# A Strassen-form decoder block in split float32: V and first group in turns, Silu on ScalarE, residuals added by DMAs

## The reference

```python
hn = rmsnorm(x, norm_g)
u_a, v_a, z_a, h_b, gb, gc, z_b = split(hn @ w_in)          # 1024 x 3584
out_a = u_a * (w_s_masked @ layernorm(v_a) + b_s) * silu(z_a)   # per chunk of 128, 4 heads
out_b = gb * causal_conv3(gc * h_b) * silu(z_b)
x = x + concat(out_a, out_b) @ w_out                         # 1024 x 1024
gate = sigmoid(rmsnorm(x, ple_norm_g) @ w_ple_gate)          # 1024 x 1024
x = x + gate * (p @ w_ple_proj)                              # 256 x 1024
out = rmsnorm(x, final_g)
```

## Time and profile before

| | |
|---|---|
| median of 3 runs | 1079.71 us (1077.2 to 1080.1) |
| the profiled execution: its time, its span | 1078.01 us, 1076.3 us |
| granted TensorE clock, mean | 0.966 of full speed |
| TensorE busy | 967.0 us (90%), 4646 matmuls |
| VectorE busy | 818.5 us (76%), 1227 instructions |
| ScalarE busy | 463.6 us (43%), 705 |
| GpSimd busy | 1.6 us, 10 |
| DMA | 94.15 MB, 87 GB/s over the span |

### The profile page before, as it was taken

The page is one execution under the profiler, slowest core; times in us unless marked ns, Lnnn a source line. Parts: engine busy times, 40 slices in busy tenths (PEclk is TensorE's granted clock), DMA queues, the critical chain, the costliest instruction groups (busy, mean ns, idle before and its releaser), DMA issues. The chain is left out here.

```text
span 1076.3 us, 12830 instructions
## 1 busy us (share of the span) xinstructions
PE 967.0 (90%) x4646; PEld 807.5 (75%) x4646; DVE 818.5 (76%) x1227; ACT 463.6 (43%) x705; POOL 1.6 (0%) x10
## 2 busy tenths in 40 slices
PE   2689999999998899889949999999999889989992
PEld 2589788888887678678749978888888767877871
DVE  3587987776779965787699898876767997578568
ACT  5454433333333414866745443333333342476351
POOL 0000000000000000000000000000000000000000
PEclk9689999999999999999979999999999999998997
DMA  9100111321213146303731122113121214510325
GB/s 304 48 1 28 52 40 40 82 75 41 78 40 118 40 156 234 145 13 117 218 134 40 43 61 55 40 53 104 40 79 40 98 59 157 194 40 1 118 79 195
DMA packets 76958, 94.15 MB, mean 87 GB/s; under 512 B 5985, under 2 KB 57697, under 8 KB 76897
## 3 DMA queue, kind: packets, MB, share of 16 engines
q1 hardware_dynamic: 76896, 93.35, 26.6%
HBM read 76.56 MB, written 16.78 MB: 87 GB/s over the span
## 5 line engine op out<-in xcount | busy, mean ns | idle before, releaser
L407 PE MATMUL banks<-ring_hi,slot 128*128 128x512 f32 (+1 forms) x672 | 248.5, 370 | 51.6 <-DVE ring_lo L1048 32.5
L1048 DVE TENSOR_TENSOR ring_lo<-work,ring_hi 128x512 fp32r<-128x512 f32 (+1 forms) x204 | 172.3, 846 | 143.8 <-ACT ring_hi L707 142.9
L407 PE MATMUL banks<-slot,ring_hi 128*128 128x512 f32 x672 | 264.3, 393 | 7.2 <-DVE work L1201 7.2
L408 PE MATMUL banks<-slot,ring_hi 128*128 128x512 f32 x672 | 261.7, 389 | 0.0
L409 PE MATMUL banks<-slot,ring_lo 128*128 128x512 f32 x672 | 261.7, 389 | 0.0
L707 ACT ACTIVATE ring_hi<-work 128x512 fp32r<-128x512 f32 (+1 forms) x204 | 153.5, 754 | 241.7 <-PE banks L409 221.8
L408 PE MATMUL banks<-ring_lo,slot 128*128 128x512 f32 (+1 forms) x672 | 244.5, 364 | 0.0
L409 PE MATMUL banks<-ring_hi,slot 128*128 128x512 f32 (+1 forms) x672 | 244.4, 364 | 0.0
L407 PEld LDWEIGHTS banks<-ring_hi,slot 128*128 128x128 f32 x672 | 132.9, 198 | 77.0 <-DVE ring_lo L1048 38.4
L407 PEld LDWEIGHTS banks<-slot,ring_hi 128*128 128x128 f32 x672 | 126.1, 188 | 39.7 <-DVE work L1201 13.9
L409 PEld LDWEIGHTS banks<-ring_hi,slot 128*128 128x128 f32 x672 | 132.5, 197 | 18.7
(11 more groups left out here) (101 smaller groups left out, 894.0 us busy)
## 6 DMA issues: line engine op xcount, KB each, us to landing
work<-in_w_in_dram SPq DMA_DIRECT2D x48, 512.0 KB, 5.1
slot_raw<-in_x_dram SPq DMA_DIRECT2D x16, 512.0 KB, 5.7
side<-in_x_dram SPq DMA_DIRECT2D x8, 1024.0 KB, 5.0
work<-in_w_out_dram SPq DMA_DIRECT2D x8, 1024.0 KB, 5.1
work<-in_w_ple_gate_dram SPq DMA_DIRECT2D x8, 1024.0 KB, 6.7
x_dram<-keep SPq DMA_DIRECT2D x16, 512.0 KB, 6.5
side<-x_dram SPq DMA_DIRECT2D x16, 512.0 KB, 3.9
out_dram<-keep SPq DMA_DIRECT2D x16, 512.0 KB, 3.0
```

The lines of the kernel that those rows point to most:

```text
L407: pe.matmul(ps, left_hi, right_hi, start=OPENS[q] and c == 0, stop=False, skip_group_check=on)
L408: pe.matmul(ps, left_hi, right_lo, start=False, stop=False, skip_group_check=on)
L1048: dve.tensor_tensor(ring_view(ring_lo, stage, place), ring_raw(stage, at, q), ring_view(ring_hi, stage, place).bitcast(F32), ALU.subtract) ...
```

## The change

- The Strassen products are signed anew: the operand's forms S1 to S4 have the same number of sums, but they are made in the order S3, S2, S4, S1, from other quarters at first (S3 = A11 - A21, S2 = A22 - S3, S4 = A12 - S2, S1 = A21 + A22), and `low_op` waits for other sums. Raw quarters lie in other slots.
- V and the first group run in turns: T(0,0), T(0,1), V0, V1, T(0,2..6), V2..6, then groups 1 to 11. The ring's places come from a table over this order (SEQ). The spatial weights move behind T(0,2) and T(0,5). The four mixing heads move to later pieces.
- V's products lie two tiles to a bank; copies and additions take 128x512 at a time, half as many.
- ScalarE computes Silu instead of Sigmoid in T (`gate_t`), VectorE drops the multiplication by z. G keeps Sigmoid.
- In O, ScalarE copies the products 0, 2, 3 (`copy_o`) and GpSimd adds x by accumulating DMAs; product 6 is still added by VectorE, to a quarter of x that SP has loaded in place. In P, x1 is added by accumulating DMAs in all 8 tiles of block 0 and in 4 of block 1; the other four are reloaded into slots.
- The weights of P have buffers of their own, outside the ring, and land in two halves. Block 1's weights and x are loaded at other points; block 0's outputs are stored by SP at the head of block 1's list.
- The last scalings (`y_tile`) are deferred: block 0's into block 1's T(0,2..5) and V2..5, block 1's to tiles 6 and 7. The two root chains of x1 become one.

The core of the diff:

```diff
-RAW_SLOT = {"A11": S2, "A12": S4, "A21": S3, "A22": A22}
+RAW_SLOT = {"A11": S3, "A12": S4, "A21": S1, "A22": A22}
-MIX_AFTER = {(2, 2): 0, (2, 6): 1, (3, 3): 2, (4, 2): 3}
+MIX_AFTER = {(2, 6): 0, (3, 2): 1, (3, 6): 2, (4, 3): 3}
+SEQ = [("T", 0, 0), ("T", 0, 1), ("V", 0), ("V", 1)] + [("T", 0, q) for q in range(2, 7)] + [("V", q) for q in range(2, 7)]
+SEQ += [("T", g, q) for g in range(1, NG) for q in range(PRODUCTS)]
+SEQ += [(stage, q, kk) for stage in "OG" for q in range(PRODUCTS) for kk in range(2)]
...
+        ADDED_BY_DMA = (8, 4)
...
             for b in range(BLOCKS):
+                if b:
+                    for i in range(TILES):
+                        sp.wait_ge(x2_step, X2("y", b - 1, i))
+                        sp.dma_start(out_tiles[b - 1, i], nat(i)).then_inc(out_stored[i], 16)
+                sp.wait_ge(w_lo_ready, W_LO("V", b, 4))
+                group_w(b, 1)
...
+                sp.wait_ge(op_lo_ready, OP_LO("mix", b, A11, 1))
+                sp.wait_ge(op_sum_ready, OP_SUM("mix", b, S3, 1))
+                sp.dma_start(nat_quarter(1, 0), x_half[b, 1][:, :, 0:HALF]).then_inc(x_quarter_landed, 16)
...
+            def add_x(b, q):                      # GpSimd's list
+                n, (t, h) = {0: (0, (0, 0)), 2: (1, (0, 1)), 3: (2, (1, 1))}[q]
+                pool.wait_ge(bank_copied, COPIED("O", b, q, 3))
+                for js in (slice(0, 2), slice(2, 4)):
+                    pool.dma_start(nat_quarter(t, h)[:, js, :], x_half[b, t][:, js, h * HALF:(h + 1) * HALF],
+                                   accum_op=ALU.add).then_inc(x_added[n], 16)
+            def add_x1(b, i):
+                pool.wait_ge(x1_stored[i], (b + 1) * 16)
+                pool.wait_ge(x2_step, X2("pp", b, i, 1))
+                pool.dma_start(nat(i), x1_tiles[b, i], accum_op=ALU.add).then_inc(x1_added[i], 16)
...
-                act.activation(sig_of(t), source, ACT.Sigmoid).then_inc(sigmoid_ready, SIGMOID.up(kind, b, i, t))
+                act.activation(gate_of(t), source, ACT.Silu).then_inc(gate_ready, GATE.up(kind, b, i, t))
...
+            def copy_o(b, q):
+                t, h = {0: (0, 0), 2: (0, 1), 3: (1, 1)}[q]
+                for s in {0: (S4,), 2: (S1, S2), 3: (S1, S3)}[q]:
+                    act.wait_ge(op_sum_ready, OP_SUM("mix", b, s, 1))
+                if q < 3:
+                    act.wait_ge(op_lo_ready, OP_LO("mix", b, A22 if q == 2 else A12, 1))
+                for j in range(4):
+                    act.wait_ge(product_done, PRODUCT("O", b, q, j))
+                    act.activation(nat(4 * t + j, h), banks[:, 4 + j if q == 3 else j, :], ACT.Copy)
...
+                gate_g(b, 1, 0)                   # ScalarE, seam
+                if b < last:
+                    for i in range(4, TILES):
+                        squares_x(b + 1, i)
+                    raw_x(b + 1, "A11")
+                    split_w(b + 1, ("T", 0, 0))
+                    raw_x(b + 1, "A12")
...
+                        if n == 5:                # VectorE, O and G
+                            add_natural(b, stage, 1)
+                        if n == 10:
+                            add_natural(b, stage, 4)
+                        if n == 12:
+                            add_natural(b, stage, 5)
...
+                        if g == 0 and q in (2, 3, 4, 5):     # VectorE, T
+                            for kk in range(2):
+                                low_op("hn", b, {2: S1, 3: S3, 4: S4, 5: A22}[q], kk)
+                        if b and g == 0 and q in (2, 4):
+                            rstd_of_squares(C_X2 + 2 * q - 4, C_X2 + 2 * q, "x2", b - 1, 2 * q - 1, q // 2 - 1)
+                        if b and g == 0 and q in (2, 3, 4, 5):
+                            y_tile(b - 1, q - 2, 0)
...
+                if i >= ADDED_BY_DMA[b]:          # x2_tile
+                    dve.wait_ge(x1_again_landed[i], 16)
+                    dve.wait_ge(x2_step, X2("pp", b, i, 1))
+                    dve.tensor_tensor(nat(i), nat(i), slot_tile(i), ALU.add).then_inc(x2_step, X2.up("sum", b, i))
```

More of the change, by code:

```diff
@@ L380, in loads @@
+            for i in range(TILES):
+                sp.wait_ge(x2_step, X2("y", last, i))
+                sp.dma_start(out_tiles[last, i], nat(i)).then_inc(out_stored[i], 16)
             for i in range(TILES):
@@ L630, in products @@
-                if b < last:
-                    x_fills(b + 1, "A11")
+                    elif stage == "O":
+                        _, q, kk = piece
+                        natural(b, "O", q, (2 * kk, 2 * kk + 1), "mix")
+                        if (q, kk) == (6, 0):
+                            x1_fills(b, "A11")
+                        if (q, kk) == (6, 1):
+                            x1_fills(b, "A12")
+                    else:
+                        _, q, kk = piece
+                        natural(b, "G", q, (2 * kk,), "x1")
+                        if (q, kk) == (0, 0):
+                            x1_fills(b, "A22")
+                        natural(b, "G", q, (2 * kk + 1,), "x1")
+                        if (q, kk) == (0, 0):
+                            x1_fills(b, "A21")
+                        if (q, kk) == (6, 0):
+                            p_fills(b)
@@ new lines, in raw_x1 @@
+            def raw_x1(b, name):
+                if b == 0 and name == "A11":
+                    act.wait_ge(const_landed, 16 * 6)
+                act.wait_ge(product_done, PRODUCT("O", b, RAW_SLOT[name], 3))
+                for c in range(4):
+                    act.wait_ge(x1t_done, X1T(b, name, c))
+                    k = 4 * QUARTERS[name][1] + c
+                    act.activation(op_raw(RAW_SLOT[name])[:, c, :], banks[:, 4 + c, :], ACT.Copy,
+                                   scale=ple_c[:, k:k + 1]).then_inc(raw_t_ready, RAW_T.up("x1", b, name, c))
@@ L860, in scalar_program @@
             act.wait_ge(pool_set, 1)
-            act.activation(warm[:, 1:2], warm[:, 0:1], ACT.Sigmoid)
+            act.activation(warm[:, 1:2], warm[:, 0:1], ACT.Silu)
             for i in range(4):
                 squares_x(0, i)
-            split_w(0, "V", 0)
-            for c in range(4):
-                raw_x(0, "A11", c)
+            split_w(0, ("T", 0, 0))
+            split_w(0, ("T", 0, 1))
+            for i in range(4, 6):
+                squares_x(0, i)
+            raw_x(0, "A11")
```

1606 lines of the change are left out of this document (765 added, 841 removed).

## The result

The changed kernel takes **1062.6 us** (median of four runs, 1060.2 to 1065.9) against 1079.9 for the kernel before on the same chip: a ratio of 0.985, 95% interval 0.982 to 0.988. It is faster, by 17 us, half of the 36 that 1044 meant. The profiled execution spans 1064.2 us, 12.1 less than the 1076.3 before.

What follows compares the result with a forecast made beforehand. TensorE's own work sets the floor; only its lost time, mostly waits for VectorE, can be won. Start -10, T -2, O -14, G -8, seam -4, end -1, table loads and hand-offs +5: -34, so 1044 us (1030 to 1056, chance 0.56).

Steps and rivals of the forecast that it cites:

- T: T stretch of each block: nearly full already, lighter gates take the waits at groups 1 and 11; -1 us per block.
- G: G stretch: 12.3 and 10.2 us lost before, waits of 1.4 and 4.5 us left; -4 us per block, near 88 each.
- O: O stretch: 10 us lost per block before, 3 left; -7 us per block, near 83 each.
- Start and end: Start: V and group 0 end about 102 us, -10. End: 22 us behind TensorE's last work, last P and end -1.
- Seam: From G's end in block 0 to V6's end in block 1: near 105 us from 108.6, -4, the least certain term.
- POOL: GpSimd's queue of added accumulating DMAs: landings of 5 to 8.6 us, priced 0; bounds 0 and 35 us.
- rival B: Accumulating DMAs come late, so the addition at half piece 10 delays TensorE; 1097 us at 35 us landing; chance 0.09.
- the sign that I had named for it: TensorE waits in O or G for x_added through VectorE's additions.
- The forecast's two waits of VectorE's order: In O: TensorE waits of about 1.6 us at O(1,1), behind copy_o, and 1.2 us at O(3,0).
- Table loads and hand-offs: ScalarE's switches between Silu and Sigmoid, four more loads for 5 us, with small hand-offs of copies and DMAs: +5 us.
- Accumulating DMAs for x1: In P, 12 of 16 additions of x1 go to DMAs, 15 us off VectorE; they land in time, cost 0.
- rival A: VectorE's queue order binds, waits fill the gaps and the seams win nothing: -15, 1063 us; chance 0.18.

Runs made afterwards that it cites:

- t_one_root: Changed kernel with V's statistics spread one to two a step and one root chain of eight columns instead of two of four: 1049.1 us (0.972).
- x1_all: Changed kernel with all eight residual tiles of the last block added by accumulating DMA, none by VectorE: 1059.5 us (0.982).
- pool_y: Changed kernel with the first block's final scaling moved from VectorE to GpSimd, as two operations per tile: 1072.4 us (0.994).

## Why the prediction was wrong, point by point

The forecast was -34 and the two profiled executions differ by -12.1. The 21.9 between them are T (+14.9), G (+7.3) and O (+6.5), less the cost that did not come (-5) and 1.8 at start and end. The steps that failed are T's, which left moved work out, and those of O and G.

- **Start and end: right. Seam: right in its number by two errors.** V and group 0 end at 101.0 (102 forecast), and 22.0 us come behind the last matmul (22). The seam takes 104.6 (105). But my walk through it adds up to 107.6 (34, then 16.6 to the 50.6, then 28 and 29), not to 105. In the trace P takes 29.2 us, not 34 (509.6 to 538.8, TensorE busy for 29.1 of them: the waits of 3 and 1.4 us for the fills did not come), and the pieces behind it 75.4 for 73.6. T(0,2) to T(0,6) take 28.7 us (28 forecast), with waits of 0.4 to 3.7 us on operand lows (slot_r).
- **T: wrong, and the largest miss.** The step was that the lighter gates "take the waits at groups 1 and 11", -1 per block. I priced what the diff took from VectorE in T and not what it moved there. By the rule that I used for every other stretch (each instruction of VectorE's queue against the piece beside it), T(1,4) alone has 5.8 us of work for 2.7. The term was +5.5 and +7.4; t_one_root, which spreads that work and drops one chain of it, takes 6.0 and 6.7 back. The gates' part was worth 3 us per block, not 1.
- **O: the mechanism right, and a wait missing.** The -7 per block is what O gives when x arrives in time (82.7 and 82.8 in three kernels, "near 83" forecast). The step that failed is POOL's: I let both halves leave at once and gave the pair one landing of 5 to 8.6 us. The second left 5.9 to 9.5 us behind the first, when that had landed, so it lands as late as 15 us behind the copy. This is rival B's place, and the sign that I had named for it did show (TensorE waits in O behind VectorE's wait for x_added), at a price of 6.0 us in block 0 and 1.4 in block 1 (88.7 and 84.2 less 82.7 and 82.8), not 26 us each. Since O's length varies between executions, the 6.0 is the price in this one. The forecast's two waits of VectorE's order (1.6 and 1.2 us) were 0.9 us or less.
- **G: mis-summed.** The 12.3 us that I called lost in block 0 hold 4.1 of the seam (see the table). And I had found waits of 1.4 and 4.5 us. The trace has 1.93 and 3.05 (4.64 in block 1) there, about the same. But my own two waits are already 6 us on top of the 82 to 84 that the matmuls need, and the slow clock behind each adds (eight matmuls at 0.43 in place of 0.23 us from 451.4, 1.6 us): that is 90 to 92, not 88. The term was -0.7 and 0, not -4.
- **Table loads and hand-offs: +5 forecast, none measured.** There were four loads, and taking three away changed nothing. ScalarE is busy 479 of 1064 us. The hand-offs in that term had no row, and no run here shows them by themselves. What the Trainium skill ("ScalarE: Activation LUTs", section What ACT_TABLE_LOAD costs) adds for a drain would have made the term larger, and this trace shows no drain; the 1.28 us of the rows stands.
- **Accumulating DMAs for x1: right.** They land in 5.4 us, and with four more at the end (x1_all) the tail is 1.6 us shorter, not longer.
- **The 1063 of rival A** is the measured time, but not by its terms: its start (-5) and seam (+2) were -11 and -4 in fact, and its T (-1 in all) was +12.9. The measured time meets its number by luck. That VectorE's order in its queue binds is right, at a place that it did not name.

The forecast of VectorE's busy time was 763 us, and 774.6 were measured: 44 us less than before, not 55. Even so the sum of the work said little about the time.

## What to carry to other kernels

When a change moves a product, list every instruction that moves with it, the statistics and root chains behind it too, and hold each step of the busiest helper engine against the length of the piece beside it; a step with twice its room costs its excess on the path, whatever the mean load. For transfers that GpSimd issues, read from the trace when the second of a pair really leaves, and cut them by tile so that each leaves when its data is ready. When work moves from a full VectorE to GpSimd, look for two prices: here GpSimd's arithmetic slowed VectorE by more than it took over, and what waited for its results in another engine's queue (the stores, and the weights behind them) came later.

## What the hardware showed that I had not expected

- The second of two accumulating DMAs of 512 KB in 2 KB rows left 5.7 to 9.7 us behind the first, and in the changed kernel 0.3 to 0.4 us after the first had landed. As 256 KB each, three left within 2.6 us and the fourth 1.8 to 2.1 us later. With 4 KB rows (x1) one was issued 0.5 us behind the end of another's issue. That the number of rows in flight is what limits it fits all three; the memory for descriptors was not varied, so this stays open.
- Beside GpSimd's arithmetic a subtraction of 128x1024 on VectorE took up to 3.4 us in place of 1.2, on tiles that the two don't share. The forecast had looked at the other direction only, VectorE in the way of GpSimd.
- In GpSimd's groups of pool_y a scaling by a column took longer (3.57 us) than the product of two tensors (2.45), the reverse of VectorE's order in the earlier trace rows (0.75 against 1.22). Both were measured beside a busy VectorE; GpSimd alone was not measured.
